# Turned up-projections and scores of 64 plus 32 partitions in the second attention path

## The chip, the core and the metric

The kernel runs on one core of a Trainium2 chip. The metric is the device time of one execution, in microseconds. The program has an instruction stream for each engine (PE for TensorE, ACT for ScalarE, DVE for VectorE, POOL for GpSimd, SP for SyncE); they are tied together by semaphores alone, and the order on each engine is written out by hand.

## What is computed

One decoder block on 256 rows of width 1024, batch 1. Two attention mixers work side by side on the normalised rows; the change concerns the second.

```python
proj = rmsnorm(x, g_mix) @ w_in          # qa, ka, va, cq, ckv, kr, gate_a, gate_b
# first path: 8 heads of 64, rotated queries and keys, causal
# second path:
qb = (rmsnorm(cq, g_cq) @ w_q_up).reshape(b, s, 8, 96)      # 64 own + 32 rotated columns a head
q_nope, q_rope = qb[..., :64], rope(qb[..., 64:])
kv = (rmsnorm(ckv, g_ckv) @ w_kv_up).reshape(b, s, 8, 128)  # 64 key + 64 value columns a head
k_nope, v_b = kv[..., :64], kv[..., 64:]
k_rope = rope(kr)                                           # one for all heads
scores = (q_nope @ k_nope.T + q_rope @ k_rope.T) * 96 ** -0.5   # causal, softmax, @ v_b
# then: gates, output projections, w_out, residual, squared-ReLU MLP of width 4096, final rmsnorm
```

The widths: cq 384, ckv 256, gates 2 x 1024.

## The kernel before

All matrices stay split into a high and a low part of a 32-bit type that TensorE multiplies in one pass; `product()` (L1410) makes one product of three matmuls, high by high, high by low, low by high. Weights come in units of up to 2048 columns into four slots of `raw`; for each half of a unit ACT writes the high part to `whi` (`high`, L546) and DVE the low part to `wlo` (`low`, L940: `raw` minus `whi`). A slot is refilled by SP when its low part is done; ACT overwrites `whi` when the products that read it are done (`used`, L310).

TensorE goes through the projections chunk by chunk: CQ, CKV, KA, QA, VA, then QB0 and QB1 (the query up-projection, four heads and 384 columns each, three tiles of contraction), KVB0 and KVB1 (keys and values, four heads and 512 columns each, two tiles), then the four gate chunks of eight tiles. In `proj` (L1426) rows of the sequence are the stationary operand (128 of them, `t` = 0 or 1) and weight columns the moving one, so a result has sequence rows on the partitions. Chunk c writes banks 2 (c mod 2) and the next one.

The latents cq and ckv are copied out of PSUM by ACT, scaled with the root of x's mean square alone, and turned by TensorE in `turn_latents` (L1477, ten transposes); ACT and DVE split them into `lat_hi` and `lat_lo` (contraction on the partitions, 256 sequence columns). Their own inverse roots, made on POOL in `inverse_root` (L463) and `scaled` (L474), are multiplied in later, when the up-projected rows leave PSUM: `up_rows` (L585) copies the 64 own columns of each head to `rows`, and the values to `v_b`; `rotate_qb` (L987) rotates the 32 others.

The rows must then be turned, since the scores contract over the head's columns. `turn_qk(e)` (L1460) does this with transposes in float32: e = 0 to 3 for the first path, 4 to 7 for the second path's queries (four transposes each, 96 partitions high), 8 to 11 for its keys (two each); `qkT_copy(e)` (L566) brings the result to `qkT_a` and `qkT_b`. The rotated key is turned once and written behind the keys of all eight heads (L688 to L692). So a head of the second path lies on 96 partitions.

In `scores(pair)` (L1593) pairs 0 to 2 are the first path, 3 to 5 the second. Pair 0 and 3 have eight heads with 128 keys, the others four heads with 256 keys. The first path's heads lie on partitions 0 to 63 and 64 to 127 alternately, and their float32 matmuls alternate between the two halves. `turn_p` (L1614) turns the probabilities, `values` (L1622) multiplies by the values. These steps are dealt out among the 32 tiles of the gate projection: `for slot in range(NGATE * KT)` at L1642. Scores stand ahead of slots 3, 8, 12, 16, 21 and 25.

Of the kernel before, what the change touches and what calls it, by code (L numbers as in the profile page):

```python
# [6 lines left out]
F32 = mybir.dt.float32  # L7
# [33 lines left out]
CQ, CKV, KA, QA, VA, QB0, QB1, KVB0, KVB1, GATE0 = range(10)  # L41
# [3 lines left out]
SHAPE = {CQ: (Q_RANK, KT), CKV: (CKV_W, KT), KA: (HALF, KT), QA: (HALF, KT), VA: (HALF, KT),  # L45
         QB0: (4 * B_QK, 3), QB1: (4 * B_QK, 3), KVB0: (HALF, 2), KVB1: (HALF, 2)}
# [5 lines left out]
UNITS_OF = {}  # L52
_u = 0
for _c in range(CHUNKS):
    _n = 2 if SHAPE[_c][1] == KT else 1
    UNITS_OF[_c] = (_u, _n, SHAPE[_c][1] // _n)
    _u += _n
U_GATE = UNITS_OF[GATE0][0]
U_WO = _u
# [21 lines left out]
QK_BANK = (7, 4, 5, 6)  # L81
Y_BANK = (2, 0, 2, 0)
# [35 lines left out]
def hybrid_block(nc, x, g_mix, w_in, b_gate, g_cq, w_q_up, g_ckv, w_kv_up, w_o_a, w_o_b, w_out,  # L118
# [10 lines left out]
    with ExitStack() as ctx:  # L129
# [19 lines left out]
        k_rope = sb("k_rope", [P, TT, B_ROPE], F32)  # L149
# [17 lines left out]
        with ExitStack() as mixer:  # L167
# [17 lines left out]
        g_fin_row = qkT_b[:, 1, 4:8, :].rearrange("p a b -> p (a b)")  # L185
        oT_hi = lat_hi[:, :, :].rearrange("p (path k) s -> p path k s", path=2)
# [40 lines left out]
        lat_rows = sem("lat_rows")  # L227
        latT = sem("latT")
# [4 lines left out]
        rows_act = sem("rows_act")  # L233
# [70 lines left out]
        ACT_READ = {CQ: (lat_rows, 2), CKV: (lat_rows, 4), VA: (act_read, 2), QB0: (rows_act, 2),  # L304
                    QB1: (rows_act, 4), KVB0: (rows_act, 6), KVB1: (rows_act, 8)}
        DVE_READ = {CKV: (krope_done, 2), KA: (rows_dve, 2), QA: (rows_dve, 4), QB0: (rows_dve, 6),
                    QB1: (rows_dve, 8)}
        DVE_READ.update({GATE0 + q: (gate_lin, TT * (q + 1)) for q in range(NGATE)})

        def used(u):  # L310

            for c in range(CHUNKS):
                first, n, _ = UNITS_OF[c]
                if first <= u < first + n:
                    if u < first + n - 1:
                        return chunk_half, 1 + sum(UNITS_OF[b][1] == 2 for b in range(c))
                    return chunk_done, TT * (c + 1)
            if u < U_OUT:
# [9 lines left out]
        def unit_source(u):  # L328

            for c in range(CHUNKS):  # L330
                first, n, kts = UNITS_OF[c]
                if first <= u < first + n:
                    k0, w = (u - first) * kts, SHAPE[c][0]
                    if c in (QB0, QB1):
                        return w_q_v[:, :, (c - QB0) * w:(c - QB0 + 1) * w]
                    if c in (KVB0, KVB1):
                        return w_kv_v[:, :, (c - KVB0) * w:(c - KVB0 + 1) * w]
                    col = {CQ: COL_CQ, CKV: COL_CKV, KA: COL_KA, QA: COL_QA, VA: COL_VA}.get(
                        c, COL_GATE + (c - GATE0) * HALF)
                    return w_in_v[:, k0:k0 + kts, col:col + w]  # L340
            if u < U_OUT:
# [5 lines left out]
        def unit_width(u):  # L347
# [3 lines left out]
            return s[1] * s[2]  # L351

# [89 lines left out]
        def _(pool):  # L442
# [35 lines left out]

            pool.wait_ge(ssq_done, 2)
# [4 lines left out]
            scaled(N_CQ, R_QB, SCALE_B)  # L484
# [1395 lines left out]
```

## Time and profile before

| | us |
|---|---|
| runs (three), median | 364.74 |
| lowest and highest | 364.2, 365.33 |
| profiled execution, first to last instruction | 363.0 |
| PE busy | 356.1 |
| PEld (weight loads) busy | 310.9 |
| DVE busy | 287.4 |
| ACT busy | 231.8 |
| POOL busy | 40.9 |

The page gives each engine's busy time, then the span in forty slices, each digit a share in tenths. A matmul's record is longer than the distance to the next one, as matmuls are pipelined; where the rate matters one reads the distance between the starts. A matmul on float32 operands shows as two instructions, so eight heads are x16. In the timeline a number behind a colon or an x counts merged instructions, and "128*128" is the size of the array that the instruction takes, rows by columns. Spans on POOL are rough.

### The profile page before, as it was taken

Reading aid. Unit: us, or ns where it says so; the run is one execution under the profiler, and the core shown is the slowest. Engines: PE = TensorE matmul, PEld = TensorE weight load, DVE = VectorE, ACT = ScalarE, POOL = GpSimd, SP = SyncE. Lnnn points to the kernel's source line nnn. Section 1 sums busy time; section 2 is a strip of 40 time slices with the busy share of each in tenths; the row PEclk is TensorE's granted clock in tenths of the full one; section 3 lists DMA queues with packets and bytes.
Section 4 is the critical chain, followed back from the end, with each engine's and each line's share of the span. In section 5 each row is a group of like instructions: output and inputs, shape, how many; then the busy total and the mean of one; then the engine's idle time right before and its main releaser. Section 6 shows DMA issues by size and latency. Waiting matters only on the chain.

```text
span 363.0 us, 5565 instructions
## 1 busy us (share of the span) xinstructions
PE 356.1 (98%) x2109; PEld 310.9 (86%) x2109; DVE 287.4 (79%) x404; ACT 231.8 (64%) x384; POOL 40.9 (11%) x62
## 2 busy tenths in 40 slices
PE   8999999999999999999999999999999999999993
PEld 7998889887788888888888899999999999999983
DVE  4877973958877777487587879999998888998584
ACT  5996436987565675064466657777677777665424
POOL 1341000000000100000021011111101111220002
PEclk9999999999999999999999999999999999999999
DMA  8999567665341366328165999999999998963003
GB/s 263 382 388 311 221 187 239 214 225 166 134 142 38 106 233 228 116 89 325 51 212 168 273 334 221 279 301 293 287 267 268 278 280 248 294 171 116 2 0 116
DMA packets 42198, 76.77 MB, mean 212 GB/s; under 512 B 1924, under 2 KB 19345, under 8 KB 41921
## 3 DMA queue, kind: packets, MB, share of 16 engines
q1 hardware_dynamic: 37840, 66.59, 53.6%
q0 software_dynamic: 4176, 9.64, 13.4%
q8 instruction: 13, 0.21, 0.2%
q10 hardware_dynamic: 160, 0.27, 0.2%
q14 instruction: 9, 0.07, 0.1%
HBM read 75.44 MB, written 1.05 MB: 211 GB/s over the span
## 4 chain that ended last, share of the span: by engine, by line
PE 96%; DMA 1%; DVE 1%; ACT 0%; issue 0%; POOLq 0%; DVEq 0%; SPq 0%; POOL 0%; ACTq 0%
PE ps L1413 29%; PE ps L1415 29%; PE ps L1414 29%; PE ps L1420 4%; PE ps L1611 2%; PE ps L1636 2%; DMA raw<-in_w_in_dram 1%; ACT prob L560 0%; PE ps L1498 0%; PE ps L1527 0%; PE ps L1522 0%; PE ps L1532 0%; DVE xs L1172 0%; POOLq L129 0%; DVE qkT_b L1403 0%
## 5 line engine op out<-in xcount | busy, mean ns | idle before, releaser
L544 ACT ACTIVATE whi<-raw 128x1024 fp32r<-128x1024 f32 (+3 forms) x127 | 119.6, 989 | 14.7 <-PE ps L1415 13.4
L944 DVE TENSOR_TENSOR wlo<-raw,whi 128x1024 fp32r<-128x1024 f32 (+2 forms) x64 | 69.9, 1127 | 25.4 <-ACT whi L544 25.3
L1413 PE MATMUL ps<-whi,xT_hi 128*128 128x512 f32 (+2 forms) x188 | 73.4, 390 | 0.0
L1415 PE MATMUL ps<-whi,xT_lo 128*128 128x512 f32 (+2 forms) x188 | 71.3, 379 | 0.0
L1414 PE MATMUL ps<-wlo,xT_hi 128*128 128x512 f32 (+2 forms) x188 | 71.2, 378 | 0.0
L1415 PE MATMUL ps<-xT_hi,wlo 128*128 128x256 f32 x224 | 63.4, 283 | 0.0
L1414 PE MATMUL ps<-xT_lo,whi 128*128 128x256 f32 x224 | 63.4, 283 | 0.0
L1413 PE MATMUL ps<-xT_hi,whi 128*128 128x256 f32 x224 | 63.3, 283 | 0.0
L1413 PE MATMUL ps<-whi,lat_hi 128*128 128x512 f32 (+2 forms) x134 | 51.7, 385 | 0.0
L1414 PE MATMUL ps<-wlo,lat_hi 128*128 128x512 f32 (+2 forms) x134 | 51.2, 382 | 0.0
L1415 PE MATMUL ps<-whi,lat_lo 128*128 128x512 f32 (+2 forms) x134 | 51.1, 382 | 0.0
L1413 PEld LDWEIGHTS ps<-xT_hi,whi 128*128 128x128 f32 x224 | 42.9, 192 | 0.6
L1414 PEld LDWEIGHTS ps<-xT_lo,whi 128*128 128x128 f32 x224 | 42.9, 192 | 0.5
L1415 PEld LDWEIGHTS ps<-xT_hi,wlo 128*128 128x128 f32 x224 | 42.9, 192 | 0.0
L1413 PEld LDWEIGHTS ps<-whi,xT_hi 128*128 128x128 f32 x188 | 35.3, 188 | 6.6 <-issue 1.0
L1415 PEld LDWEIGHTS ps<-whi,xT_lo 128*128 128x128 f32 x188 | 35.3, 188 | 6.5
L1414 PEld LDWEIGHTS ps<-wlo,xT_hi 128*128 128x128 f32 x188 | 35.4, 188 | 5.6
L1210 DVE TENSOR_TENSOR wlo<-raw,whi 128x1024 fp32r<-128x1024 f32 x28 | 33.9, 1218 | 0.5 <-ACT whi L544 0.5
L544 ACT ACTIVATE t_hi<-t_raw 128x1024 fp32r<-128x1024 f32 (+1 forms) x24 | 20.0, 838 | 19.0 <-DVE t_raw L1224 19.0
L1415 PEld LDWEIGHTS ps<-whi,lat_lo 128*128 128x128 f32 x134 | 25.2, 188 | 4.7
L1413 PEld LDWEIGHTS ps<-whi,lat_hi 128*128 128x128 f32 x134 | 25.2, 188 | 4.0
L1414 PEld LDWEIGHTS ps<-wlo,lat_hi 128*128 128x128 f32 x134 | 25.3, 188 | 4.0
(157 smaller groups left out, 499.9 us busy)
## 6 DMA issues: line engine op xcount, KB each, us to landing
raw<-in_w_ff_dram SPq DMA_DIRECT2D x32, 1024.0 KB, 7.2
raw<-in_w_in_dram SPq DMA_DIRECT2D x14, 1024.0 KB, 6.3
raw<-in_w_out_dram SPq DMA_DIRECT2D x4, 1024.0 KB, 5.1
t_raw<-in_w_ff_dram SPq DMA_DIRECT2D x12, 256.0 KB, 7.9
raw<-in_w_ff_dram POOLq DMA_DIRECT2D x12, 256.0 KB, 4.8
t_raw<-in_w_ff_dram POOLq DMA_DIRECT2D x12, 256.0 KB, 7.2
gates<-in_b_gate_dram POOLq DMA_DIRECT2D x2, 1024.0 KB, 6.8
raw<-in_w_o_a_dram SPq DMA_DIRECT2D x2, 1024.0 KB, 5.1
```

The lines of the kernel that those rows point to most:

```text
L544: return nc.scalar.activation(dst, src, ACT.Copy, scale=scale)
L944: nc.vector.tensor_tensor(wlo[:, s, h * w:(h + 1) * w], raw[:, s, h * w:(h + 1) * w], whi[:, s, h * w:(h + 1) * w].bitcast(F32), ALU.subtr ...
L1210: nc.vector.tensor_tensor(wlo[:, s, h * w:(h + 1) * w], raw[:, s, h * w:(h + 1) * w], whi[:, s, h * w:(h + 1) * w].bitcast(F32), ALU.subtr ...
L1413: nc.tensor.matmul(dst, a_hi, b_hi, start=start, stop=False)
L1414: nc.tensor.matmul(dst, a_hi, b_lo, start=False, stop=False)
L1415: return nc.tensor.matmul(dst, a_lo, b_hi, start=False, stop=stop)
L1420: m = nc.tensor.transpose(ps[0:width, bank, b * P:(b + 1) * P], src, ident[:, :])
L1611: m = nc.tensor.matmul(dst, q[:, t * P:(t + 1) * P], k[:, 0:keys], start=True, stop=True)
L1636: m = nc.tensor.matmul(ps[h % 2 * 64:h % 2 * 64 + 64, O_BANK, h // 2 * P:(h // 2 + 1) * P], v[:, kb, h * 64:(h + 1) * 64], prob[:, 2 + g % ...
```

## The change

The up-projections of the second path are no longer four chunks of `proj`. Three things come in their place.

- The own query columns and the key columns are computed turned: in `own_parts` the weights (128 columns, two heads) are the stationary operand and the 256 sequence columns of the latents the moving one. The result has head columns on the partitions, two heads at a time, and ACT copies it to `qn_T` and `kn_T` as it is. To this end `up_part` lets ACT and DVE write the own columns of a unit ahead of the others.
- The rotated query columns of all eight heads are one product for each block of sequence rows (`last_parts`, 256 columns from two units); so are the values (512 columns). DVE rotates 256 columns at once; `turn_rotated` turns them with four transposes, ahead of slot 3. The rotated key is written to two places, partitions 0 to 31 and 32 to 63.
- In `scores` a head of the second path takes a matmul on 64 partitions and then, adding to the same PSUM columns, one on 32 partitions; the heads come two by two, first both 64-partition matmuls, then both 32-partition ones.

The inverse roots of cq and ckv are now multiplied in before `turn_latents`: POOL scales the four row tiles in place (`normed`), and `turn_latents` waits for `lat_normed` to be 4. The rotation and the copies behind the up-projections have no factor any more. GATE0 changes its number from 9 to 5 and uses the same banks.

```diff
+            def normed(rows_of, col):
+                pool.wait_ge(rstd_done, n_rstd[0])
+                for t in range(TT):
+                    pool.tensor_scalar(rows_of[:, t, :], rows_of[:, t, :], rstd[:, col + t:col + t + 1], None,
+                                       ALU.mult).then_inc(lat_normed, 1)
...
             scaled(N_CQ, R_QB, SCALE_B)
+            normed(cq_rows, R_QB)
             pool.wait_ge(ssq_done, 6)
             inverse_root(ssq[:, N_CKV:N_CKV + TT], N_CKV, TT, KV_RANK)
+            normed(ckv_rows, N_CKV)
...
             high_unit(13)
-            up_both(QB0)
+            q_own(0)
+            q_own(1)
             high_unit(14)
-            up_both(QB1)
             high_unit(15)
-            qkT_copy(4)
-            qkT_copy(5)
-            up_both(KVB0)
+            k_own(0)
+            k_own(1)
             high_unit(16)
-            qkT_copy(6)
-            qkT_copy(7)
...
-            up_both(KVB1)
-            qkT_copy(8)
-            qkT_copy(9)
-            qkT_copy(10)
-            high(U_GATE + AHEAD, 0)
-            qkT_copy(11)
-            high(U_GATE + AHEAD, 1)
+            v_rows(0)
+            v_rows(1)
+            high_unit(U_GATE + AHEAD)
+            q_rotated()
...
             low_unit(13)
-            dve.wait_ge(rstd_done, RSTD_QB)
-            rotate_qb(QB0)
+            rotate_q(0)
+            rotate_q(1)
             low_unit(14)
-            rotate_qb(QB1)
             low_unit(15)
...
+            def own_parts(u, k_tiles, k0, bank, done):
+
+                pe.wait_ge(wlo_ready, 2 * u + 1)
+                for b in range(2):
+                    for k in range(k_tiles):
+                        w = slice(k * OWN + b * P, k * OWN + (b + 1) * P)
+                        m = product(ps[:, bank, b * SEQ:(b + 1) * SEQ], whi[:, u % SLOTS, w], wlo[:, u % SLOTS, w],
+                                    lat_hi[:, k0 + k, :], lat_lo[:, k0 + k, :], k == 0, k == k_tiles - 1)
+                m.then_inc(done, 1)
+
+            def last_parts(u, k_tiles, n, k0, banks, done):
+
+                pe.wait_ge(wlo_ready, 2 * u + 4)
+                s = u % SLOTS
+                for t in range(TT):
+                    for k in range(k_tiles):
+                        a = (slice(None), k0 + k, slice(t * P, (t + 1) * P))
+                        w = slice(k_tiles * OWN + k * n, k_tiles * OWN + (k + 1) * n)
+                        m = product(ps[:, banks[t], 0:2 * n].rearrange("p (u n) -> p u n", u=2), lat_hi[a], lat_lo[a],
+                                    whi[:, s:s + 2, w], wlo[:, s:s + 2, w], k == 0, k == k_tiles - 1)
+                    m.then_inc(done, 1)
+
+            def up_queries():
+                pe.wait_ge(rows_dve, 2 * TT)
+                for i in range(2):
+                    own_parts(U_QB + i, 3, 0, QN_BANK[i], qn_done)
+                pe.wait_ge(act_read, TT)
+                last_parts(U_QB, 3, 4 * B_ROPE, 0, QR_BANK, qr_done)
+
+            def up_keys():
+                pe.wait_ge(qkT_ready, 2)
+                for i in range(2):
+                    own_parts(U_KVB + i, 2, 3, KN_BANK[i], kn_done)
+                pe.wait_ge(rows_dve, 3 * TT)
+                last_parts(U_KVB, 2, 4 * B_V, 3, VB_BANK, vb_done)
+
+            def turn_rotated():
+                pe.wait_ge(qkT_ready, 4)
+                turn(QR_TURNED, [rows[:, t, b * P:(b + 1) * P] for b in range(2) for t in range(TT)], P, qr_turned)
 
             def turn_latents():
-                pe.wait_ge(lat_rows, 4)
+                pe.wait_ge(lat_normed, 4)
...
             proj_all(VA, 6)
-            proj_all(QB0)
-            proj_all(QB1)
-            turn_qk(4)
-            turn_qk(5)
-            proj_all(KVB0)
-            turn_qk(6)
-            turn_qk(7)
-            proj_all(KVB1)
+            up_queries()
+            up_keys()
...
-                for i, h in enumerate(heads):
-                    dst = ps[:, S_BANK + i % 2, i // 2 * keys:(i // 2 + 1) * keys]
-                    if path == 0:
-                        b = h % 2 * A_DIM
-                        q, k = (qkT_a[b:b + A_DIM, w, h // 2, :] for w in range(2))
-                    else:
-                        q, k = (qkT_b[0:B_QK, w, h, :] for w in range(2))
-                    m = nc.tensor.matmul(dst, q[:, t * P:(t + 1) * P], k[:, 0:keys], start=True, stop=True)
+                for i in range(0, len(heads), 2):
+                    cols, rows_of = slice(i // 2 * keys, (i // 2 + 1) * keys), slice(t * P, (t + 1) * P)
+                    for h in heads[i:i + 2]:
+                        b = slice(h % 2 * A_DIM, h % 2 * A_DIM + A_DIM)
+                        q, k = (qkT_a[b, w, h // 2, :] for w in range(2)) if path == 0 else \
+                            (w[b, h // 2, :] for w in (qn_T, kn_T))
+                        m = nc.tensor.matmul(ps[:, S_BANK + h % 2, cols], q[:, rows_of], k[:, 0:keys], start=True,
+                                             stop=(path == 0))
+                    for h in heads[i:i + 2] if path == 1 else ():
+                        b = slice(h % 2 * B_ROPE, (h % 2 + 1) * B_ROPE)
+                        m = nc.tensor.matmul(ps[:, S_BANK + h % 2, cols], qr_T[b, h // 2, rows_of], kr_T[b, 0:keys],
+                                             start=False, stop=True)
                 m.then_inc(scored, 1)
...
             for slot in range(NGATE * KT):
-                if slot in (1, 2):
-                    turn_qk(6 + 2 * slot)
-                    turn_qk(7 + 2 * slot)
+                if slot == SCORE_SLOT[0]:
+                    turn_rotated()
```

The waits added elsewhere: `scores(0)` for `kn_ready` 1, `scores(3)` for `qn_ready` 2, `kn_ready` 2 and `qr_ready` 1, `turn_p(0)` for `qr_ready` 1, `values(0)` for `kn_ready` 2, `values(3)` for `vb_ready` 2, the first two gate chunks for `qn_ready` 2 and `vb_ready` 2. `used` releases the slots of units 10 and 11 at `qr_done` 2 and those of 12 and 13 at `vb_done` 2.

## Rows read from the trace of the kernel before

**Rows 1.** The page: span, busy time of PE, granted clock, engines of the chain.
```profile
span 363.0 us, 5565 instructions
PE 356.1 (98%) x2109; PEld 310.9 (86%) x2109; DVE 287.4 (79%) x404; ACT 231.8 (64%) x384; POOL 40.9 (11%) x62
...
PEclk9999999999999999999999999999999999999999
...
PE 96%; DMA 1%; DVE 1%; ACT 0%; issue 0%; POOLq 0%; DVEq 0%; SPq 0%; POOL 0%; ACTq 0%
```

**Rows 2.** Windows: from:to, us, busy PE PEld DVE ACT POOL, clock, DMA share, GB/s.
```profile
36.96:41.50 4.54, 4.54 (x22) 3.76 (x21) 4.37 (x10) 1.72 (x3) 0.00 (x0) 1.00 0.94 360
58.39:64.66 6.27, 6.27 (x38) 6.22 (x36) 3.86 (x11) 5.10 (x9) 0.00 (x0) 1.00 0.56 178
61.89:64.06 2.17, 2.17 (x14) 2.17 (x14) 1.97 (x8) 2.17 (x3) 0.00 (x0) 1.00 0.76 180
```

**Rows 3.** Timeline of PE (start, us, engine, line): query products, transposes, key and value products.
```profile
58.39 0.33 PE L1413 MATMUL ps<-whi,lat_hi 128*128 128x384 f32 x1
...
64.66 1.04 PE L1420 MATMUL ps<-ident,rows 128*96 128x128 f32 x8
...
65.76 0.39 PE L1414 MATMUL ps<-wlo,lat_hi 128*128 128x512 f32 x1
...
68.28 1.04 PE L1420 MATMUL ps<-ident,rows 128*96 128x128 f32 x8
```

**Rows 4.** Timeline of PE in the MLP: first of 48 products of 256 columns, and the next form.
```profile
245.51 0.28 PE L1413 MATMUL ps<-xT_hi,whi 128*128 128x256 f32 x1
...
251.26 0.40 PE L1413 MATMUL ps<-whi,lat_hi 128*128 128x512 f32 x1
```

**Rows 5.** Timeline of PE around scores(0), on 64 partitions.
```profile
76.70 0.40 PE L1415 MATMUL ps<-whi,xT_lo 128*128 128x512 f32 x1
77.03 1.16 PE L1611 MATMUL ps<-qkT_a 64*128 64x128 f32 x16
78.12 0.50 PE L1413 MATMUL ps<-whi,xT_hi 128*128 128x512 f32 x1
78.46 0.39 PE L1414 MATMUL ps<-wlo,xT_hi 128*128 128x512 f32 x1
```

**Rows 6.** Timeline of PE at scores(3) and scores(4), on 96 partitions, with values() behind.
```profile
103.31 1.95 PE L1611 MATMUL ps<-qkT_b 96*128 96x128 f32 x16
105.19 1.09 PE L1636 MATMUL ps<-prob,v_a 128*64 128x128 f32 x16
...
114.06 1.89 PE L1611 MATMUL ps<-qkT_b 96*128 96x256 f32 x8
115.88 1.09 PE L1636 MATMUL ps<-prob,v_b 128*64 128x128 f32 x16
```

**Rows 7.** Timeline of PE at the transposes of gains and latents.
```profile
30.23 0.39 PE L1415 MATMUL ps<-whi,xT_lo 128*128 128x512 f32 x1
30.55 0.22 PE L1566 MATMUL ps<-ident,grow_lat 5*128 5x5 f32 x1
30.70 1.31 PE L1420 MATMUL ps<-ident,gates 128*128 128x128 f32 x10
```

**Rows 8.** Timelines of POOL (four rows) and of DVE (two).
```profile
18.53 1.11 POOL L475 TENSOR_SCALAR rstd<-rstd 128x2 f32<-128x2 f32 x1
...
26.88 0.19 POOL L465 TENSOR_SCALAR var<-ssq 128x2 f32<-128x2 f32 x1 [3.25 <-ACT prob L560]
27.16 0.71 POOL L469 TENSOR_TENSOR rstd<-var,neg_half 128x2 f32<-128x2 f32 x1
...
316.30 3.39 POOL L521 TENSOR_SCALAR qkT_b<-qkT_b 128x1024 f32<-128x1024 f32 x1
...
18.33 2.36 DVE L944 TENSOR_TENSOR wlo<-raw,whi 128x1024 fp32r<-128x1024 f32 x2 [1.13 <-ACT whi L544]
28.44 2.35 DVE L944 TENSOR_TENSOR wlo<-raw,whi 128x1024 fp32r<-128x1024 f32 x2
```

More of the change, by code:

```diff
@@ L38 @@
 COL_GATE = COL_CKV + CKV_W
-CQ, CKV, KA, QA, VA, QB0, QB1, KVB0, KVB1, GATE0 = range(10)
+CQ, CKV, KA, QA, VA, GATE0 = range(6)
 NGATE = 2 * D // HALF
 CHUNKS = GATE0 + NGATE
-SHAPE = {CQ: (Q_RANK, KT), CKV: (CKV_W, KT), KA: (HALF, KT), QA: (HALF, KT), VA: (HALF, KT),
-         QB0: (4 * B_QK, 3), QB1: (4 * B_QK, 3), KVB0: (HALF, 2), KVB1: (HALF, 2)}
+SHAPE = {CQ: (Q_RANK, KT), CKV: (CKV_W, KT), KA: (HALF, KT), QA: (HALF, KT), VA: (HALF, KT)}
 SHAPE.update({GATE0 + n: (HALF, KT) for n in range(NGATE)})
@@ L51 @@
 SLOT_W = 2048
[L52 to L59, printed above, removed]
+U_QB = 2 * GATE0
+U_KVB = U_QB + 2
+U_GATE = U_KVB + 2
+UNITS_OF = {_c: (2 * _c if _c < GATE0 else U_GATE + 2 * (_c - GATE0), 2, KT // 2) for _c in range(CHUNKS)}
+U_WO = U_GATE + 2 * NGATE
 U_OUT = U_WO + 4
@@ L81 @@
 QK_BANK = (7, 4, 5, 6)
+QN_BANK = (2, 3)
+QR_BANK = (0, 1)
+KN_BANK = (4, 7)
+VB_BANK = (0, 1)
+QR_TURNED = 6
+OWN = 4 * B_NOPE
 Y_BANK = (2, 0, 2, 0)
@@ L232, in hybrid_block @@
         rows_dve = sem("rows_dve")
-        rows_act = sem("rows_act")
+        qn_done = sem("qn_done")
+        qn_ready = sem("qn_ready")
+        qr_done = sem("qr_done")
+        qr_turned = sem("qr_turned")
+        qr_ready = sem("qr_ready")
+        kn_done = sem("kn_done")
+        kn_ready = sem("kn_ready")
+        vb_done = sem("vb_done")
+        vb_ready = sem("vb_ready")
         krope_done = sem("krope_done")
@@ L301, in hybrid_block @@
         out_stored_act = sem("out_stored_act")
[L304 to L307, printed above, removed]
+        ACT_READ = {CQ: (lat_rows, 2), CKV: (lat_rows, 4), QA: (qn_ready, 2), VA: (vb_ready, 2)}
+        DVE_READ = {CKV: (krope_done, 2), KA: (rows_dve, 2)}
         DVE_READ.update({GATE0 + q: (gate_lin, TT * (q + 1)) for q in range(NGATE)})
@@ L956, in _, with rotate @@
             n_rot = [0]
-            def rotate(src, dst, tab, t, r, heads, dim, tmp_a, tmp_b, done, before):
+            def rotate(src, dst, tab, t, r, heads, dim, tmp_a, tmp_b, done, before, copies=1):
                 if before:
@@ new lines, in turn_qk @@
+                pe.wait_ge(rows_dve, e + 1)
+                turn(QK_BANK[e], blocks(rows[:, e, :]), P, qk_turned)
+            def own_parts(u, k_tiles, k0, bank, done):
[6 more added lines that the diff above has]
+                m.then_inc(done, 1)
```

146 lines of the change are left out of this document (70 added, 76 removed).

## The prediction

> **What bounds the kernel now.** I read the page first. TensorE is busy for 356.1 of 363.0 us, and the chain of work that ended last lies on it for 96% of the span [rows 1]. So a microsecond of TensorE's own stream is a microsecond of the kernel, and work taken off the other engines is worth nothing by itself. The granted clock is 0.9 or more in every slice, so it is at the upper of its levels (2.4 GHz) and durations from different stretches can be compared [rows 1]. Then I read the stretch that the change touches, by the table of windows: from 58.39 to 64.66 us, where the query up-projection runs, PE is busy 6.27 of 6.27 us while DVE and ACT have gaps [rows 2]. There is no stall to remove here; only the length of the stream can change. The third view is the timeline of PE, read for start-to-start distances, since the durations of pipelined matmuls overlap: a 384-column product takes (64.66 - 58.39) / 36 = 0.174 us; a 512-column one (68.28 - 65.76) / 11 = 0.229 us (eleven products start in that time); a 256-column one (251.26 - 245.51) / 48 = 0.120 us [rows 3, 4].
>
> The sum is made against the profiled execution, 363.0 us from first to last instruction. The median of the runs is 364.74, so 1.7 us lie outside the span; I carry them over unchanged.
>
> **Up-projection products.** Removed: 36 of 384 columns (QB0, QB1) and 24 of 512 (KVB0, KVB1), 36 x 0.174 + 24 x 0.229 = 6.27 + 5.49 = 11.76 us. Added: own_parts, 36 + 24 products of 256 columns; last_parts for the rotated queries, 18 of 256 columns; last_parts for the values, 12 of 512. That is 78 x 0.120 + 12 x 0.229 = 9.36 + 2.75 = 12.11 us. The columns streamed are the same in number, and the short products pay their fixed part more often: **+0.35 us**, all of it on the path.
>
> **Transposes.** turn_qk(4) to turn_qk(7) are 16 transposes and turn_qk(8) to turn_qk(11) are 8. Eight cost 0.87 us: the transposes start at 64.66, and the first product behind them, whose recorded start is early, streams from 65.76 - 0.229 = 65.53 [rows 3]. That is 0.109 each, with nothing lost going in or out. 24 go and 4 (turn_rotated) come: 20 x 0.109 = **-2.18 us**. The two transposes of k_rope stay two.
>
> **Scores of the second path.** Before, eight heads with 128 keys (x16 in the profile, two instructions for a float32 matmul) take 105.19 - 103.31 = 1.88 us up to the values in their 64-column form. 0.09 us of this is the emptying of the array at a change of form (the size of it comes from rows 7, below), 1.79 is stream, 0.112 an instruction. Four heads with 256 keys take 115.88 - 114.06 = 1.82, stream 1.73, and there are two such groups [rows 6]. Stream in all 5.25 us. Afterwards the 64-partition parts run as the first path's do, two heads side by side on the two halves of the rows. There the trace shows 16 instructions between 77.03 and 78.12 [rows 5]: half of 1.79 is 0.90 of stream. The 32-partition parts also come in pairs, on partitions 0 to 31 and 32 to 63, at the same columns. So the stream is half of 5.25 for the one and half for the other: 5.25 again, **no gain and no loss in the stream itself**.
>
> What is added is the change of array form. The last product before scores(0) starts at 76.70 and would be streamed at 76.93; the scores start at 77.03. The second product behind them starts at 78.46, so the first streams from 78.23. Between 76.93 and 78.23 lie 1.30 us, of which 0.90 are stream: 0.40 us for going into the 64-row form and out of it, **0.20 us for each change** [rows 5]. It is an emptying of the array (about 0.1) and then a weight load that nothing hides (about 0.1). The 96-partition matmuls pay nothing on entry: at 103.31 they follow the product before at its usual distance. Leaving them for the 64-column form of values() costs what leaving a row-tiled form costs, so the exits stay as they are. Now the code of scores(): for each pair of heads it issues two 64-row matmuls, then two 32-row ones. With 128 keys that is 8 segments, 1 entry and 7 inner changes; with 256 keys 4 segments, 4 changes, twice. That is 16 changes that were not there, 16 x 0.20 = **+3.2 us**, on the path, because PE has no idle time there.
>
> Of the 16, three are the entry that is measured. The other 13 are changes between 64 and 32 rows, which no row shows. The nearest is the transpose of the latent gains: five rows high, it starts at 30.55 where the product of 30.23 would be streamed at 30.46, so a small form behind a full one also waits 0.09 us before its weight load starts [rows 7]. Bounds for an inner change: nothing (the array treats both as row-tiled and loads the next weights meanwhile) and 0.20 us. I take 0.20, as the measured entry and exit and the small form agree. The Trainium skill has the rule for this (TensorEngine Tiling (Array Packing), section Key Properties): changing the tiling mode, as opposed to the tile within a mode, drains the engine. By that rule each inner change drains too; the trace agrees for full-to-64 and full-to-small forms, and no run here yet shows 64-to-32.
>
> **Scaling of the latents, moved to POOL.** Before, the rows are scaled on the way out of PSUM; now POOL multiplies cq_rows (2 x 384 wide) and ckv_rows (2 x 256) in place, and turn_latents waits for all four. Queued behind it on PE are the rest of KA and everything after. PE starts those transposes at 30.70, and the last inverse root starts at 27.16 on POOL and, 0.7 us long, ends at 27.87 [rows 7, 8]. Bounds for one 256-wide multiplication: above, a quarter of the 1024-wide one of 3.39 us, 0.85 us; below, the two-element one of 0.19 us at 26.88 [rows 8]. Two take 0.4 to 1.7 us, so they end between 28.3 and 29.6, at least 1.1 us early: **nothing on the path**. What can spoil it is DVE. The two-element scaling at 18.53 took 1.11 us instead of 0.19, up to 19.64. DVE had started two wlo subtractions, which read two SBUF operands, at 18.33; they take 1.18 each, so the first ended at 19.51 [rows 8]. POOL was held for the length of a DVE instruction. DVE runs such subtractions from 28.44 on, exactly then [rows 8]. This is a rival below. The skill (SBUF — State Buffer, section SBUF: two separate sides) says the same: a DVE op with two SBUF inputs and a GpSimd op that reads SBUF exclude each other for a whole instruction; the trace agrees.
>
> **ACT and DVE.** ACT loses the row copies and the copies behind removed transposes and gains eight PSUM copies (two each for the own queries, the own keys, the values and the rotated queries); DVE does two rotations of 256 columns instead of four of 128. ACT and DVE are off the path, so this is costed at nothing. The cover is thinnest at last_parts of the values, which waits for both rotations (rows_dve 6), with the whole GATE0 stage queued behind it. On the new stream the queries' last parts end at 58.39 + 54 x 0.120 = 64.87, the keys' own parts at 64.87 + 24 x 0.120 = 67.75. A pair of 512-wide rotations takes 4.54 us, a pair of 128-wide 2.17 [rows 2]; in between, a 256-wide pair takes 2.96. It can start when the first row block is done, at 63.79 plus some 0.2 for the way out of the array (a 512-column product's record is 0.39 us long at a distance of 0.229), and ends at 67.0 to 67.3: about 0.45 us to spare. The other new waits (kn_ready before scores(0), qr_ready before turn_p(0), vb_ready before gate chunk 1) stand behind ACT copies that come microseconds earlier by the same reckoning. The releases of slots 2 and 3 move to the end of the query stage and those of slots 0 and 1 to the end of the value stage, at 67.75 + 2.75 = 70.5; the units that want them are not multiplied before GATE0 is half done, 5.5 us later or more. No SP load is ordered differently.
>
> **Sum.** +0.35 - 2.18 + 3.2 = +1.37 us: span 364.4, time 364.74 + 1.37 = **366.1 us**.
>
> **Rivals.**
> A. *Cheap inner changes; faster than before.* The 13 changes between 64 and 32 rows cost nothing and only the 3 entries do. Then 0.35 - 2.18 + 0.6 = -1.2 us, time 363.5. For it: both are row-tiled forms, and within the row-tiled stretch at 77.03 loads run beside matmuls. Against it: the 0.09 us wait before the five-row form. The point from which the change gains is an inner change below (2.18 - 0.35 - 0.6) / 13 = 0.09 us.
> B. *Half price.* An inner change shows only the weight load, 0.1 us: 0.6 + 1.3 + 0.35 - 2.18 = +0.1 us, time 364.8, no difference.
> C. *The latents are late.* POOL's multiplications each wait for a DVE subtraction of 1.2 us. Two of them and 0.4 to 1.7 us of work from 27.87 give 30.7 to 32.0 against 30.70: up to 1.3 us of stall, taken as 0.7. On top of the forecast: 366.8. The same place would show the multiplications of cq_rows delaying DVE's subtractions. For it: the 1.11 us row. Against it: just ahead of 28.44 DVE has only the short k_rope steps.
> D. *The 32-row matmuls don't run side by side.* Their stream is then 5.25 instead of 2.63: 368.7. Nothing but the 64-row pairs speaks on it, and these do run side by side.
>
> **How the numbers follow.** Forecast 0.50, A 0.15, B 0.10, C 0.20, D 0.05. A measurement of this kernel can tell about 0.3%, 1.1 us. The forecast's +1.37 is only a little above that, so I give it 0.34 for slower and 0.16 for the same; with C and D slower is 0.59. B is the same, and a little of A (its 1.2 us is near the bound, too): same 0.29, faster 0.12. The range leaves out D and the far end of C above and about half of A below: 363.5 to 367.4.
>
> **What would show it.** In the profile after: 78 products at 0.120 us; PE groups of L1420 24 transposes fewer and 4 more; the scores of the second path at 3.3 to 3.4 us for eight heads and 2.5 for four, with PE weight loads starting 0.09 us after the array is empty at each change of row count. If those groups take 2.3 and 2.1 us, A holds. If PE idles just ahead of the transposes of the latents, with POOL named, C holds; if it idles before the values' last parts with DVE rows named, my 0.45 us of slack was wrong. The prediction is wrong altogether if an inner change costs less than 0.09 us.

## The result, and the profile after

| | before | changed |
|---|---|---|
| median of the runs, side by side | 364.61 us | 368.78 us (four runs: 367.93, 368.05, 369.52, 369.61) |
| ratio | | 1.0115, 95% interval 1.0098 to 1.0131 |
| profiled execution, span | 363.0 us | 366.2 us |

The changed kernel is slower, by 4.17 us of the medians. The prediction said slower by 1.4 us (366.1, range 363.5 to 367.4): the direction is right, the size is wrong, and the measured time lies outside the range. Nothing in the page of the changed kernel looks like a new bottleneck. It answers to [rows 1]: PE is as busy as before and the clock is as high, but POOL has entered the chain that ended last, with 3% of the span, and ACT, which stands ahead of POOL in it, has 3%, too.

```profile
span 366.2 us, 5610 instructions
PE 357.2 (98%) x2151; PEld 309.8 (85%) x2151; DVE 285.4 (78%) x396; ACT 225.4 (62%) x367; POOL 48.8 (13%) x66
...
PEclk9999999999999999999999999999999999999998
...
PE 90%; ACT 3%; POOL 3%; issue 1%; DMA 1%; DVE 0%; SPq 0%; POOLq 0%; DVEq 0%; ACTq 0%
```

Why POOL is there is seen in the timeline of PE at the transposes of the latents, the stretch of [rows 7]:

```profile
30.41 0.22 PE L1609 MATMUL ps<-ident,grow_lat 5*128 5x5 f32 x1
32.76 1.31 PE L1435 MATMUL ps<-ident,gates 128*128 128x128 f32 x10 [2.12 <-POOL gates L506]
33.82 0.48 PE L1428 MATMUL ps<-whi,xT_hi 128*128 128x512 f32 x1
```

The transposes followed the five-row one after 0.15 us before; now they follow it after 2.35 us, and the bracket names who released them: POOL's L506, the new multiplications. The timelines of POOL and of DVE at that place answer to [rows 8]:

```profile
23.65 4.66 POOL L506 TENSOR_SCALAR gates<-gates,rstd 128x384 f32<-128x384 f32 x2
28.39 0.19 POOL L489 TENSOR_SCALAR var<-ssq 128x2 f32<-128x2 f32 x1
...
29.57 3.13 POOL L506 TENSOR_SCALAR gates<-gates,rstd 128x256 f32<-128x256 f32 x2 [0.18 <-POOL rstd L493]
...
28.73 2.35 DVE L961 TENSOR_TENSOR wlo<-raw,whi 128x1024 fp32r<-128x1024 f32 x2
```

Two things are to be seen. The 256-wide pair takes 3.13 us, where the prediction had 0.4 to 1.7. And it starts late: the 384-wide pair is in the queue ahead of it until 28.31, so the last inverse root begins at 28.39 where it began at 26.88.

The timeline adds up what stands next to each other. The view by source line has the two multiplications of the pair apart (shortest, median and longest in ns, then the start of the first and of the last):

```profile
L506 POOL TENSOR_SCALAR gates<-gates,rstd x2: 917/1574/2230, 29.6 to 31.8; 128x256 f32<-128x256 f32 x2
```

The first takes 2.23 us. It ends at 31.80, 0.7 us behind DVE's last subtraction (28.73 + 2.35 = 31.08). The second, with DVE quiet, takes 0.92.

The rest went as predicted. PE's timeline in the turned projections, in place of [rows 3]: the first own query product, the first own key product, the first value product, and the first product behind them; then the last transposes and scores(0).

```profile
60.47 0.28 PE L1428 MATMUL ps<-lat_hi,whi 128*128 128x256 f32 x1
...
66.95 0.28 PE L1428 MATMUL ps<-lat_hi,whi 128*128 128x256 f32 x1
...
69.83 0.40 PE L1428 MATMUL ps<-whi,lat_hi 128*128 128x512 f32 x1
...
72.57 0.39 PE L1428 MATMUL ps<-whi,xT_hi 128*128 128x512 f32 x1
...
76.66 0.60 PE L1435 MATMUL ps<-ident,rows 128*128 128x128 f32 x4
77.19 1.16 PE L1651 MATMUL ps<-qkT_a 64*128 64x128 f32 x16
```

From 60.47 to 72.57 lie 12.10 us (the prediction: 12.11), and there is no gap ahead of the values. scores(0) began at 77.03 [rows 5] and begins at 77.19, although the stall had put the query products 2.08 us later (60.47 against 58.39): 1.92 us were gained between, against 2.18 - 0.35 = 1.83 predicted.

The scores of the second path, in place of [rows 6]:

```profile
103.24 0.40 PE L1430 MATMUL ps<-whi,xT_lo 128*128 128x512 f32 x1
103.56 0.49 PE L1651 MATMUL ps<-qkT_b 64*128 64x128 f32 x4
103.98 0.49 PE L1655 MATMUL ps<-qkT_b 32*128 32x128 f32 x4
...
106.93 1.09 PE L1682 MATMUL ps<-prob,v_a 128*64 128x128 f32 x16
...
115.93 0.70 PE L1651 MATMUL ps<-qkT_b 64*128 64x256 f32 x4
116.56 0.70 PE L1655 MATMUL ps<-qkT_b 32*128 32x256 f32 x4
...
118.46 1.09 PE L1682 MATMUL ps<-prob,v_b 128*64 128x128 f32 x16
```

Each segment of four instructions takes 0.42 us with 128 keys and 0.63 with 256: eight heads 3.37 us instead of 1.88, four heads 2.53 instead of 1.82 (there are two such groups). That is 1.49 + 2 x 0.71 = +2.91 us from the first score instruction to the first behind them. Ahead of each group the array is emptied, which was not needed before: 103.56 - 103.24 - 0.23 = 0.09 us, three times. In all +3.18 us, where the prediction had +3.2.

So the two profiled executions should differ by 2.05 (the stall, from the first product behind the transposes: 33.82 against 31.77) - 1.92 + 3.18 = 3.3 us; the spans differ by 366.2 - 363.0 = 3.2. (The stall itself is 2.2 us, 2.35 - 0.15; the changed kernel reached the five-row transpose 0.14 us earlier, 30.41 against 30.55.) The stream alone, without the stall, costs 1.26 us: my sum said 1.37. What is wrong with the prediction is what it costed at nothing. That leaves about 0.9 us of the 4.17, and the four runs show where to look: two are at 368.0 and two at 369.6. The median lies between them.

### The profile page after: what moved, and what is told of

Same layout as the page of the kernel before. It is cut to its first block, busy times and chain, and to the rows that moved or that the text cites. A ratio compares the mean times of both kernels' runs of the same rounds, so it can differ in the third digit from the quotient of the medians.

```text
span 366.2 us, 5610 instructions
## 1 busy us (share of the span) xinstructions
PE 357.2 (98%) x2151; PEld 309.8 (85%) x2151; DVE 285.4 (78%) x396; ACT 225.4 (62%) x367; POOL 48.8 (13%) x66
## 4 chain that ended last, share of the span: by engine, by line
PE 90%; ACT 3%; POOL 3%; issue 1%; DMA 1%; DVE 0%; SPq 0%; POOLq 0%; DVEq 0%; ACTq 0%
PE ps L1428 27%; PE ps L1430 27%; PE ps L1429 27%; PE ps L1435 4%; POOL gates L506 2%; PE ps L1651 2%; PE ps L1682 2%; ACT whi L576 1%; DMA raw<-in_w_in_dram 1%; PE ps L1655 1%; ACT xT_hi L576 1%; ACT prob L596 0%; POOL rstd L493 0%; ACT rows L596 0%; POOL rstd L499 0%
## 5 line engine op out<-in xcount | busy, mean ns | idle before, releaser
L961 DVE TENSOR_TENSOR wlo<-raw,whi 128x1024 fp32r<-128x1024 f32 (+1 forms) x56 | 64.9, 1193 | 16.1 <-ACT whi L576 16.1
L1428 PE MATMUL ps<-whi,lat_hi 128*128 128x512 f32 (+1 forms) x124 | 47.6, 384 | 0.0
L1429 PE MATMUL ps<-wlo,lat_hi 128*128 128x512 f32 (+1 forms) x124 | 47.4, 382 | 0.0
L1430 PE MATMUL ps<-whi,lat_lo 128*128 128x512 f32 (+1 forms) x124 | 47.3, 381 | 0.0
L1430 PEld LDWEIGHTS ps<-whi,lat_lo 128*128 128x128 f32 x124 | 23.3, 188 | 4.5
L1429 PEld LDWEIGHTS ps<-wlo,lat_hi 128*128 128x128 f32 x124 | 23.4, 189 | 3.8
L1428 PEld LDWEIGHTS ps<-whi,lat_hi 128*128 128x128 f32 x124 | 23.4, 189 | 3.8
```

What stands on the lines that cost most here:

```text
L961: nc.vector.tensor_tensor(wlo[:, s, h * w:(h + 1) * w], raw[:, s, h * w:(h + 1) * w], whi[:, s, h * w:(h + 1) * w].bitcast(F32), ALU.subtr ...
L1428: nc.tensor.matmul(dst, a_hi, b_hi, start=start, stop=False)
L1429: nc.tensor.matmul(dst, a_hi, b_lo, start=False, stop=False)
L1430: return nc.tensor.matmul(dst, a_lo, b_hi, start=False, stop=stop)
```

## The experiments

The theory to be tested (S): the loss is two separate things, 16 changes of array form at about 0.2 us (less the shorter projections), and a stall at the transposes of the latents that comes from POOL's multiplications. Rivals: the stall is hidden anyway by something later (H); the turned projections or the scores hold a cost that the two profiles hide (K). Within the stall, there are three possible causes: POOL's multiplication is slow in itself with a factor read from memory (F); POOL is held by DVE's subtractions (D, the mechanism of rival C); the 384-wide pair blocks POOL's queue (Q).

**The changed kernel once more.** No edit.

> The changed kernel, nothing altered, to see whether its four times (two near 368.0, two near 369.6) are two levels and in which interval the extra 1.6 us lie. Theory P (the latents are late on POOL): the stall before the transposes of the latents is 2.1 us in every execution, and in the longer ones it is longer by one more POOL or DVE instruction (1.2 to 1.6 us). Rival: the extra time lies in the MLP part, behind 165 us. Expected 368 to 369.6 us, ratio to the kernel before 1.009 to 1.013.

Measured: 369.18 us, ratio 1.0111 [1.0081, 1.0141]; the four runs are 368.13, 368.39, 369.97 and 370.01, two levels again. This time a profile caught the upper one (span 368.2). The extra time is in neither of the two places that I expected: the stall is 2.21 us where it was 2.12, with POOL's and DVE's instructions as long as before, and the MLP has no part in it. The page's clock row has an 8 where the others have a 9, and windows and PE's timeline show what it is:

```profile
PEclk9998999999999999999999999999999999999998
```

```profile
34.17:38.00 3.83, 3.83 (x13) 3.01 (x11) 2.90 (x6) 3.82 (x7) 1.18 (x2) 0.55 0.68 227
```

```profile
33.10 1.32 PE L1435 MATMUL ps<-ident,gates 128*128 128x128 f32 x10 [2.21 <-POOL gates L506]
34.17 0.68 PE L1428 MATMUL ps<-whi,xT_hi 128*128 128x512 f32 x1
34.65 0.63 PE L1429 MATMUL ps<-wlo,xT_hi 128*128 128x512 f32 x1
...
37.90 0.40 PE L1428 MATMUL ps<-whi,xT_hi 128*128 128x512 f32 x1
```

PE stood idle for 2.21 us, did its transposes, and then the granted clock was 0.55 on the mean of 3.83 us (the lower level, 1.2 GHz, for nearly all of it; behind the window and its length stand PE, PEld, DVE, ACT, POOL, clock, DMA share, GB/s). 512-column products start 0.43 us apart instead of 0.23. From 34.17 to 37.90 nine of them take 3.73 us, where the same nine take 2.16 at the upper level (in the version that follows, 32.17 to 34.33): 1.6 us lost. The two levels of the runs lie 1.6 to 1.7 us apart. The stall has a second price that comes in some executions only. In the first profile, behind 2.12 us of idle time, the same window has a granted clock of 1.00.

**Scaling on ACT.** The four multiplications leave POOL and stand on ACT, around the copies of unit 7:

```
-            normed(cq_rows, R_QB)
...
-            normed(ckv_rows, N_CKV)
...
+            def normed(rows_of, col, ready):
+                act.wait_ge(rstd_done, ready)
+                for t in range(TT):
+                    copy(rows_of[:, t, :], rows_of[:, t, :], rstd[:, col + t:col + t + 1]).then_inc(lat_normed, 1)
+
+            normed(cq_rows, R_QB, RSTD_QB)
             high_unit(7)
+            normed(ckv_rows, N_CKV, RSTD_CKV)
```

> The four multiplications of the latents by their inverse roots are done on ACT instead of POOL, the rest of the change stays. ACT takes 0.5 us for 384 columns and 0.4 for 256, so the last ends near 29.8 us, ahead of PE's 30.5. Theory P: the stall of 2.1 us goes, span 366.2 - 2.2 = 364.0, time about 365.9 (ratio 1.0035), and what is left, +1.2 to +1.4 us, is the sum of the prediction. Rival: the stall comes from something else that turn_latents waits for, and the time stays near 368.

Measured: 366.54 us (366.23 to 366.69, one level), ratio 1.0048 [1.003, 1.0067], span 364.5. PE's timeline and ACT's:

```profile
30.89 0.22 PE L1614 MATMUL ps<-ident,grow_lat 5*128 5x5 f32 x1
31.11 1.31 PE L1440 MATMUL ps<-ident,gates 128*128 128x128 f32 x10
...
27.25 1.11 ACT L574 ACTIVATE gates<-gates,rstd 128x384 f32<-128x384 f32 x2
...
30.16 0.89 ACT L574 ACTIVATE gates<-gates,rstd 128x256 f32<-128x256 f32 x2
```

The stall is gone, and so is the upper level of the runs: H falls. The same multiplications take ACT 2.0 us in all, and POOL 7.8. They end at 31.05, later than the 29.8 that I expected, just as TensorE gets there: its transposes follow 0.22 us behind the five-row one, instead of 0.15. What is left is 1.5 us by the spans, of which 0.34 is a later start (the five-row transpose is at 30.89 instead of 30.55); the rest, 1.2, is the stream. The medians have 1.95, with an interval of 1.1 to 2.4 that takes in the stream's 1.26.

**Mirrored scores.** Every second pair of heads issues its 32-partition part first, so that two parts of the same form meet and the changes of form fall from 16 to 11 (5 instead of 8 with 128 keys, twice 3 instead of 4 with 256):

```
+                    own_first = i // 2 % 2 == 0
+                    for own in (own_first, not own_first) if path == 1 else (True,):
+                        for h in heads[i:i + 2]:
...
```

> The changed kernel with the order inside the second path's scores mirrored for every second pair of heads (own, rotated, rotated, own), so that there are 5 + 3 + 3 = 11 changes of array form instead of 16. Theory S (0.20 us for each change, 64 to 32 rows too): scores with 128 keys 3.38 - 0.6 = 2.8 us, with 256 keys 2.53 - 0.2 = 2.3 us each, in all -1.0 us against the changed kernel. Rival: the 0.42 us of a four-instruction segment is a fixed price of the 32-row matmuls and not of the change, and nothing is gained.

Measured: 367.26 us, ratio 1.0079 [1.0049, 1.011], span 365.5; the stall is still there (2.4 us). PE's timeline:

```profile
103.80 2.85 PE L1658 MATMUL ps<-qkT_b 64*128 64x128 f32 x32
106.58 1.09 PE L1686 MATMUL ps<-prob,v_a 128*64 128x128 f32 x16
...
115.55 2.40 PE L1658 MATMUL ps<-qkT_b 64*128 64x256 f32 x16
117.88 1.09 PE L1686 MATMUL ps<-prob,v_b 128*64 128x128 f32 x16
```

2.78 us instead of 3.37 for three changes fewer, 2.33 instead of 2.53 for one fewer: 0.20 us a change. The times agree: three of the four runs lie at 366.9 to 367.3, 1.1 us below the lower level of the changed kernel beside them (368.1 and 368.4); the fourth, 368.83, has a mean clock of 0.992. Between 64 and 32 partitions the array pays what it pays between 128 and 64. The Trainium skill's rule (TensorEngine Tiling (Array Packing), section Key Properties: "Changing tiling mode (not just tile) drains the TensorE") holds here for a change between two row-tiled forms too.

**Both.** Mirrored scores and scaling on ACT.

> The changed kernel with both repairs: latents multiplied on ACT, and the scores of every second pair in mirrored order, so 11 changes of array form instead of 16. If the two costs are separate and add, the span is that of the ACT version (364.5 us) less five changes of 0.2 us, 363.5 us, and the ratio to the kernel before is 1.001 to 1.003. If the scores' gain is lost beside the ACT version's timing, it stays at 364.5 us and 1.005.

Measured: 365.24 us, ratio 1.0015 [1.0005, 1.0024], span 363.3, as expected. The two costs are separate and add up. PE's timeline shows one more thing:

```profile
30.80 1.31 PE L1440 MATMUL ps<-ident,gates 128*128 128x128 f32 x10 [0.63 <-ACT gates L574]
```

In this execution TensorE reached the five-row transpose at 29.95 and waited for ACT's last multiplication until 30.75. So the scaling on ACT has no slack either. What is left of the loss, 0.2 to 0.9 us by the interval, is covered by the stream (1.26 less five changes of 0.20) and this wait; K has nothing to explain.

**Before, with POOL's scaling alone.** The kernel before, with normed() on POOL, turn_latents waiting for it, and factor 1.0 at the later places; nothing else changed.

> The kernel before with one part of the change alone: POOL scales the latents ahead of turn_latents, the factor at the copies of the up-projected rows becomes one. Theory P: the whole price of this part appears without the rest, PE idles 2.1 to 2.4 us before the transposes of the latents, span 363.0 + 2.2 = 365.2, in some executions 1.6 more by a lower granted clock behind the idle stretch: ratio 1.006 to 1.010. Rival: the stall needs the rest of the change, then 1.000.

Measured: 368.66 us, ratio 1.0124 [1.0109, 1.014], span 366.7. This one edit, put into the kernel before, loses as much as the whole change loses on the median. POOL's timeline and PE's:

```profile
28.75 1.79 POOL L470 TENSOR_TENSOR rstd<-var,neg_half 128x2 f32<-128x2 f32 x1
30.72 2.08 POOL L483 TENSOR_SCALAR gates<-gates,rstd 128x256 f32<-128x256 f32 x2 [0.18 <-POOL rstd L470]
...
32.85 2.39 PE L1429 MATMUL ps<-ident,gates 128*128 128x128 f32 x10 [2.09 <-POOL gates L483]
```

Here DVE's subtractions began at 28.74, a moment ahead of the root, and the root took 1.79 us instead of the 0.7 that it has elsewhere: it is a two-element instruction held for a whole subtraction. The pair behind it then took 2.08 us, not 3.13. The stall was 2.09 and the clock was at its lower level right behind it (the ten transposes take 2.39 us, and 1.31 elsewhere); all four runs have a mean clock of 0.992 or 0.993, below every execution without a stall (0.995 to 0.999), so all four paid the second price. The stall of 2.2 us and 1.6 for the clock make the 3.7 by which the span is longer. That is why my expectation, which took it as the exception, was 1.5 us too low.

**Is it POOL's multiplication itself (F)?** The factor read from memory is replaced by the constant 1.0. This leaves the scaling of the latents out, so that the kernel computes something else.

```
-                    pool.tensor_scalar(rows_of[:, t, :], rows_of[:, t, :], rstd[:, col + t:col + t + 1], None,
+                    pool.tensor_scalar(rows_of[:, t, :], rows_of[:, t, :], 1.0, None,
```

> The changed kernel with the factor of POOL's four multiplications given as a constant 1.0 instead of a column of roots: it leaves out the scaling of the latents, and nothing else. It measures what the form of the operand costs. The prediction's bound came from a multiplication by a constant, 3.4 us for 1024 columns (3.3 ns a column); the changed kernel's took 2.33 us for 384 and 1.57 for 256 (6.1 ns a column). Theory F (the column operand costs the double): 1.2 to 1.3 us for 384 and 0.85 for 256, stall near 0. Rival D (POOL is held up by DVE's two-operand subtractions): unchanged 2.3 and 1.6.

Measured: span 364.5, one execution. POOL's timeline:

```profile
23.76 3.46 POOL L506 TENSOR_SCALAR gates<-gates 128x384 f32<-128x384 f32 x2
...
28.64 2.46 POOL L506 TENSOR_SCALAR gates<-gates 128x256 f32<-128x256 f32 x2 [0.17 <-POOL rstd L493]
```

3.46 instead of 4.66 us and 2.46 instead of 3.13, and the stall is down to 0.34 us. Both expectations fail. F, a multiplication that is slow in itself with a factor from memory, falls: the first of the 256-wide pair, which ran mostly ahead of DVE's subtraction of 29.17, takes 0.86 us, and with the factor and DVE quiet it takes 0.93 (next experiment). The second, beside the subtractions, takes 1.63, and DVE's own become longer here: 1.52 us for two of the four beside the 384-wide pair and 1.42 for one of the later two, where in the changed kernel one takes 1.53 and the others 1.22. So the constant removes 1.8 of the 2.1 us of stall, more than either edit below, nearly all of it by a shorter hold; why POOL is held less, no run shows.

**Is it DVE's subtractions (D)?** DVE waits with the low half of unit 7 until the latents are scaled:

```
+            dve.wait_ge(lat_normed, 4)
             low_unit(7)
```

> The changed kernel with DVE's low_unit(7) held back until POOL's four multiplications are done, so that no two-operand subtraction of DVE runs beside the last two. Theory F (POOL's own rate): the 256-column multiplications still take 1.57 us each, the stall stays at 2.1 us. Rival D (held by DVE): they fall to 0.85 or less each and the stall to 0.7.

Measured: span 364.8, one execution. Timelines of POOL, DVE and PE:

```profile
29.44 1.83 POOL L506 TENSOR_SCALAR gates<-gates,rstd 128x256 f32<-128x256 f32 x2 [0.18 <-POOL rstd L493]
...
31.31 2.36 DVE L961 TENSOR_TENSOR wlo<-raw,whi 128x1024 fp32r<-128x1024 f32 x2 [2.49 <-POOL gates L506]
...
31.33 1.31 PE L1436 MATMUL ps<-ident,gates 128*128 128x128 f32 x10 [0.76 <-POOL gates L506]
```

With DVE quiet the same pair with the same factor takes 1.83 us instead of 3.13 (0.93 and 0.92 for the two, where it was 2.23 and 0.92): 3.6 ns a column. (The 384-wide pair, beside whose subtractions nothing was changed, still took 4.65.) DVE's hold is 1.30 of the 3.13 us, and without it the stall is 0.76.

**Is it the queue (Q)?** The 384-wide pair goes to ACT, the 256-wide one stays on POOL.

> The changed kernel with the two 384-wide multiplications of the queries' latents on ACT and only the two 256-wide ones on POOL. In the changed kernel the 256-wide pair begins at 29.57 us, behind a backlog that the 384-wide pair left (it delayed its root from 26.88 to 28.39 us), and takes 3.13 us. Theory 'backlog': the root is again done at about 27.9 us, the 256-wide pair ends at about 31.0 us, and TensorE waits 0.3 to 0.6 us ahead of turn_latents instead of 2.1: span about 364.8 us, about 0.3 above the version with all four on ACT. Theory 'the pair's own length alone': the stall stays near 2 us and the span near 366.2 us. If the fall of TensorE's clock that follows the stall in some executions needs the long stall, none of these executions shows it.

Measured: 367.4 us, ratio 1.0091 [1.0062, 1.012], span 365.3; the four runs have spans of 365.3, 365.5, 365.5 and 367.5, and only the last has a mean clock of 0.992. Timelines of POOL, DVE and PE:

```profile
28.05 3.82 POOL L506 TENSOR_SCALAR gates<-gates,rstd 128x256 f32<-128x256 f32 x2 [0.19 <-POOL rstd L493]
...
28.79 2.36 DVE L963 TENSOR_TENSOR wlo<-raw,whi 128x1024 fp32r<-128x1024 f32 x2 [0.19 <-ACT whi L575]
...
31.92 1.31 PE L1437 MATMUL ps<-ident,gates 128*128 128x128 f32 x10 [1.30 <-POOL gates L506]
```

The view by source line, as above:

```profile
L506 POOL TENSOR_SCALAR gates<-gates,rstd x2: 940/1916/2892, 28.0 to 29.0; 128x256 f32<-128x256 f32 x2
```

The pair starts 1.5 us earlier, and then takes 0.7 us longer. The first multiplication is through at 28.99 after 0.94 us; the second starts at 28.97, just behind the first subtraction, and takes 2.89, to 0.7 us behind the end of both (28.79 + 2.36 = 31.15). The pair is held 3.82 - 1.83 = 1.99 us instead of 1.30. Of 1.5 us that the free queue gives, the hold takes back half. My expectation of 0.3 to 0.6 us of stall had overlooked this, and the other one (no fall of the clock) failed too: by its time and mean clock it fell in one of four executions. The trace with 1.30 us of idle time is of another one; how long TensorE stood in this one is not on record. Neither Q nor D is the cause alone: the stall of 2.12 us is 0.76 with DVE held back, 1.30 with the queue free, and 0.34 with both there and a constant factor.

**A version with what is good in the change.** The turned projections stay, the latents are scaled on ACT, and the heads are put together again on 96 partitions, so that the scores are those of before:

```
+            def own(which, i, bank, done, ready):
...
+                    m = copy(qkT_b[0:B_NOPE, which, 4 * i + odd:4 * i + 4:2, :],
...
+                for j in range(4):
+                    m = copy(qkT_b[B_NOPE:B_QK, 0, j:8:4, :], ps[j * B_ROPE:(j + 1) * B_ROPE, QR_TURNED, :]
```

> Turned up-projections as in the change, scaling of the latents on ACT, but each head is put together on 96 partitions again (ACT copies own parts and rotated parts below one another; the scores are those of the kernel before). No row-tiled changes in the second path, 20 transposes less than before. Theory: 363.0 - 2.18 + 0.35 = 361.2 us span, time about 362.9, ratio 0.995 to the kernel before: faster than both. Rival: the ACT copies (8 of 64 partitions, 4 of 32, about 0.55 us each) come too late for scores(0) or exps, and PE waits; then 362 to 364 us of span.

Measured: 363.76 us (8 runs), ratio 0.9974 [0.9963, 0.9985], span 361.4: faster than both, though the time that I expected was 362.9. PE's timeline and ACT's show what it pays:

```profile
81.57 0.60 PE L1445 MATMUL ps<-ident,prob 128*128 128x128 f32 x4
82.52 0.66 PE L1445 MATMUL ps<-ident,prob 128*128 128x128 f32 x4 [0.35 <-DVE prob L1115]
82.93 0.48 PE L1438 MATMUL ps<-whi,xT_hi 128*128 128x512 f32 x1
...
76.20 2.40 ACT L572 ACTIVATE qkT_b<-ps 32x512 f32<-32x512 f32 x4
```

Four copies of 32 partitions take ACT 2.40 us just ahead of the first softmax, which then keeps turn_p(0) waiting: it takes 1.36 us to the next product, and 0.79 where nothing holds it. A last version moves the copies of the values behind that point:

> Experiment e4 (turned up-projections, scaling on ACT, heads on 96 partitions) with the two value copies of ACT (1.1 us) moved from ahead of the first exponentials to behind the first pair's. In e4 ACT worked without a gap from 64.9 us to the end of the first exponentials, and PE waited 0.57 us for the first turned probabilities. Theory: that wait goes, span 361.4 - 0.5 = 360.9, ratio about 0.993 to 0.996. Rival: gate chunk 1 now waits for the value copies and PE loses as much there.

Measured: 363.38 us (7 runs), ratio 0.9972 [0.9961, 0.9983], span 361.4. The span was expected at 360.9. The wait at turn_p(0) is gone (0.79 us from its start to the next product), but at the next transposes, at 90.56, 0.26 us are lost that were not before. The gain over the version ahead of it is within the intervals: not shown.

## Why the prediction was wrong, point by point

- **Bound and projections: right.** 12.10 us against 12.11, transposes and products together -1.92 against -1.83. The slack ahead of the values' last parts, put at 0.45 us, was 1.08 (DVE's last rotation ended at 68.75, the parts began at 69.83); PE doesn't wait there.
- **Scores: right.** 0.20 us for each change is confirmed by the mirrored order, and the total was +3.18 where 16 x 0.20 gave 3.2. Rivals A, B and D fall: a segment of either form takes 0.42 us, of which 4 x 0.056 is stream and 0.20 the change. The sum of +1.37 met a stream that costs 1.26.
- **Scaling of the latents, costed at nothing: the step that failed.** "Two take 0.4 to 1.7 us, so they end between 28.3 and 29.6, at least 1.1 us early" ended at 32.70, and TensorE stood for 2.1 us. The upper bound of 0.85 us for one is nearly right for POOL alone (0.92 and 0.93), but it was used where DVE subtracts: there the first takes 2.23. And the row that it was scaled from (316.30, 3.39 us) was itself beside a subtraction, DVE's L1240 at 316.51; only there it was DVE that became longer, 1.97 us against a median of 0.69 for that line:

```profile
L1240 DVE TENSOR_TENSOR t_lo<-t_raw,t_hi x12: 682/691/1973, 207.6 to 327.4; 128x512 fp32r<-128x512 f32 x12
```

The sum also left out what is queued: the 384-wide pair holds POOL until 28.31, so the root that I read at 26.88 came 1.51 us later. The two together are the whole miss, by an estimate from two runs: a pair that starts at 28.05 (queue free) and takes 1.83 us (DVE quiet) ends at 29.88, ahead of the transposes; no run has both on POOL. DVE may stand behind the queue, too: at the 3.6 ns a column of the quiet pair, the 384-wide one would take 2.8 us instead of 4.66, and end before 26.88. The prediction had the 1.11 us row and gave it to rival C, with 0.20; the queue it didn't look at, and named the 384-wide multiplications only as something that may delay DVE. That they did as well: the four subtractions beside them take 4.94 us instead of 4.63. "Just ahead of 28.44 DVE has only the short k_rope steps" was true and beside the point, since the pair ran into the subtractions from whichever side it started.
- **Rival C was what happened**, above its own bounds: its worst end was 32.0 and a stall of 1.3, its price 0.7; measured were 32.70 and 2.1. It had each multiplication wait for one subtraction, and no queue ahead; in fact one of the two waited for what was left of both subtractions, from 29.57 to 31.08, and the other for none.
- **A fall of the clock was not thought of.** A stall of PE was priced as its length. In two of four executions of the second measurement (and, by their times alone, perhaps in two of the first), 1.6 us came on top, which moves the median by about half of that. The sum of the parts is then 1.26 + 2.05 + 0.8 = 4.1, against 4.17 measured; that the last part has this cause is shown for the second measurement only.

**What stays open.** What decides whether the clock falls: it fell, by time and mean clock of each execution, in 8 of 16 of the versions with a stall of 1.3 us or more (2 of 4, 1 of 4, 1 of 4, and 4 of 4 for the kernel before with POOL's scaling), and in none of the 29 executions of the four versions that do all the scaling on ACT. The length of the idle stretch alone doesn't decide it: in the traces it fell behind 2.09 and 2.21 us, and not behind 2.12 and 2.38 (the mirrored scores). The two longer runs of the first measurement have 0.994 and 0.995 as their mean clock, against 0.995 in the shorter ones, and no trace. The mean clock can't decide it: each profile has the lower level at the very end of the span as well, when TensorE is done, for 0.4 us in the kernel before and 3.7 in the changed one, which moves the mean as much as a fall would. That the same fall made these two longer is likely from the size of the step, and not shown. Why POOL is held less with a constant factor, one execution can't tell. What holds the median of the best versions 0.2 to 0.5 us above their profiled executions was not looked into.

## What to carry to other kernels

When a step moves to another engine's queue, write down that queue as a list with start times: what stands ahead of the step, what stands behind it, and which two-operand instructions of DVE run beside it on SBUF; here, of a stall of 2.1 us, 0.8 went with the queue and 1.4 with DVE's subtractions, and the slack was thought to be 1.1. Ask when the last of those subtractions ends, not only how long POOL's instruction is: the first multiplication that it held was through 0.7 us behind it. The same scaling on ACT took 2.0 us instead of 7.8, and cost TensorE nothing in two profiles, 0.07 us in one and 0.6 in one, so it stands at the edge, too. A sum of the stream can be right to 0.1 us and the forecast still miss by nearly three, because the price of an edit costed at nothing isn't bounded by its own length.

## What the runs showed of the hardware

- POOL, multiplication of 128 x 256 float32 by a factor per partition: 0.92 or 0.93 us with DVE quiet, 2.23 and 2.89 where it met DVE's subtractions of two SBUF operands, each time to 0.7 us behind the end of the last of them; a root of two elements 0.73 us or 1.79. The Trainium skill describes this (SBUF — State Buffer, section SBUF: two separate sides): whichever starts first gets the shared pair of ports for the whole instruction, and the other fully blocks. The traces agree for POOL behind DVE. They don't bear out the other direction: the multiplication of 28.05 to 28.99 didn't lengthen the subtraction that began at 28.79 (1.23 us), and the one of 316.30 to 319.69 held a subtraction only until 318.48. Spans on POOL are rough, so this is an observation and no rule.
- DVE's subtractions of 1024 columns take 1.22 us, and up to 1.53 beside POOL's multiplications; one of 512 columns 0.69, and 1.97.
- A change between 64-row and 32-row matmuls costs 0.20 us, no less than one between full and 64-row form.
- TensorE's granted clock fell to the lower level for about 3.4 us behind an idle stretch of 2.1 or 2.2 us (two traces), in some executions and not in others of the same kernel, at a price of 1.6 us.
